# Round u slices dealt 5, 8, 8, a block's exponentials between the two last of a round, value products by turns and decay columns over four strips

## What is computed

```python
p_pool, gq, gk, gv, gg, gz_f, gz_b, aq, ak, av = _split_proj(h @ w_in)
la_f = _gla_log_decay(gz_f, gla_w_f, gla_b_f)      # log_sigmoid(gz_f @ w + b) / 16, gz_f and gz_b 16 columns each
y_attn = softmax over keys, then p @ v             # 8 heads, 2 key heads, window of 3 blocks and a cached one
mix = jnp.concatenate([y_pool, y_gla, y_attn], axis=-1)
x = x + gt1 * (mix @ w_out)
h2 = _rmsnorm(x, n2) * (1 + sc2) + sh2
# PEER: q = h2 @ wq; scores with subkeys; top 16 of 256 pair sums for each of 8 heads
gates = jax.nn.softmax(top_v, axis=-1)
act = gelu(einsum('td,tkd->tk', h2, u[experts]))
x = x + gt2 * einsum('tk,tkd->td', gates * act, v[experts])
```

## Time and profile before

| | |
|---|---|
| median of 3 runs | 3841.5 us (3837.81 to 3842.62) |
| the profiled execution | 3839.85 us |
| its span | 3838.0 us |
| PE busy | 3654.0 us, 95% |
| DVE, POOL, ACT busy | 2597.6, 1635.7, 699.3 us |
| mean granted clock | 0.983 |

### The profile page before, as it was taken

The page is one execution under the profiler, slowest core; times in us unless marked ns, Lnnn a source line. Parts: engine busy times, 40 slices in busy tenths (PEclk is TensorE's granted clock), DMA queues, the critical chain, the costliest instruction groups (busy, mean ns, idle before and its releaser), DMA issues. The chain is left out here.

```text
span 3838.0 us, 39960 instructions
## 1 busy us (share of the span) xinstructions
PE 3654.0 (95%) x13726; PEld 2084.1 (54%) x13726; DVE 2597.6 (68%) x6024; ACT 699.3 (18%) x1575; POOL 1635.7 (43%) x1498
## 2 busy tenths in 40 slices
PE   5888989999999999999989899899999999999997
PEld 3456776655555555554455567665555555555543
DVE  7784879977667667677624748899777555565444
ACT  1152366300000000000013425661000000000000
POOL 0210155466566544444402003554877564444330
PEclk9989999999999999999999999999999999999999
DMA  6323045799999999999830122558999999899774
GB/s 270 104 90 116 19 141 149 253 368 389 381 369 377 379 376 371 376 375 361 347 125 2 68 105 73 148 152 299 407 410 410 379 346 368 341 357 356 293 299 156
DMA packets 365049, 1026.96 MB, mean 268 GB/s; under 512 B 30352, under 2 KB 132016, under 8 KB 364208
## 3 DMA queue, kind: packets, MB, share of 16 engines
q0 software_dynamic: 147456, 536.94, 36.5%
q1 hardware_dynamic: 118352, 436.07, 29.7%
q10 hardware_dynamic: 99040, 51.40, 4.9%
HBM read 965.07 MB, written 59.22 MB: 267 GB/s over the span
## 5 line engine op out<-in xcount | busy, mean ns | idle before, releaser
L1860 PE MATMUL ps<-colsT,arena 128*128 128x384 f32 x4096 | 1370.1, 489 | 4.3 <-DMA arena<-in_peer_ut 4.3
L1860 PEld LDWEIGHTS ps<-colsT,arena 128*128 128x128 f32 x4096 | 780.6, 191 | 585.9 <-issue 104.1
L1896 PE MATMUL ps<-arena 128*128 128x512 f32 x1536 | 676.5, 592 | 0.0
L1388 POOL DMA_INDIRECT proj<-in_peer_u,eidx x336 | 476.5, 1418 | 240.3 <-DVE modbc L1573 106.0
L1388 POOL DMA_INDIRECT proj<-in_peer_v,eidx x335 | 359.9, 1074 | 316.4 <-DVE colsT L1584 217.2
L1896 PEld LDWEIGHTS ps<-arena 128*128 128x128 f32 x1536 | 291.8, 190 | 345.2 <-issue 317.6
L1374 POOL TENSOR_SCALAR x<-iota,modbc 128x128 f32<-128x128 f32 x192 | 145.3, 772 | 692.2 <-ACT modbc L1699 550.2
L1573 DVE CUSTOM_DVE_ANT_0 proj<-proj,rows 128x1024 f32<-128x1024 f32 x336 | 399.6, 1223 | 57.7 <-DMA proj<-in_peer_u,eidx 55.7
L1584 DVE SCALAR_TENSOR_TENSOR colsT<-proj,modbc,colsT 128x1024 f32<-128x1024 f32 x330 | 409.6, 1286 | 14.2 <-DMA proj<-in_peer_v,eidx 14.1
L1388 POOL DMA_INDIRECT modbc<-in_peer_v,eidx x177 | 200.4, 1132 | 325.8 <-DVE colsT L1584 259.7
L1896 PE MATMUL ps<-arena,rows 128*128 128x512 f32 x768 | 337.8, 592 | 0.0
(11 more groups left out here) (293 smaller groups left out, 3736.8 us busy)
## 6 DMA issues: line engine op xcount, KB each, us to landing
arena<-in_peer_ut SPq DMA_DIRECT2D x256, 512.0 KB, 6.8
arena<-in_peer_v SPq DMA_DIRECT2D x256, 512.0 KB, 6.7
gmat_d<-arena ACTq DMA_DIRECT2D x24, 2048.0 KB, 10.1
arena<-gmat_d SPq DMA_DIRECT2D x64, 768.0 KB, 9.0
proj<-in_w_adaT SPq DMA_DIRECT2D x51, 512.0 KB, 9.3
modbc<-in_w_adaT SPq DMA_DIRECT2D x19, 512.0 KB, 9.0
rows<-in_w_adaT SPq DMA_DIRECT2D x18, 512.0 KB, 3.5
arena<-in_w_in SPq DMA_DIRECT2D x2, 4224.0 KB, 16.3
```

Of the source, the lines that this page charges most:

```text
L1388: pool.indirect_dma_start(ring[slots[at]], None, tab, bass.IndirectOffsetOnAxis(ap=eidx[:, b * SLOTS + q:b * SLOTS + q + 1], axis=0)).then ...
L1860: mm = pe.matmul(ps[:, 2 + j % 2, 0:ND], utab[:, j % UR, k], hT[:, k, NG:T], start=(k == 0), stop=(k == KT - 1))
L1896: mm = pe.matmul(ps[:, Y_BANKS[2 * d + c2], :], wT[j % CR][:, d * P:(d + 1) * P], vtab[:, j % VR, c2 * 512:(c2 + 1) * 512], start=(j == 0) ...
```

## The change

Five edits.

1. `gz` is no longer made by `columns` but by `decay_columns`: k tile k goes to the strip of 32 output columns 32 (k % 4), so that four partial sums over two k tiles each stand in the four quarters of PSUM's partitions. `gzT` and `gw2` are 128 partitions high; `gw2` holds the weights four times, so the logits' matmul adds the four parts.
2. `values` takes the key blocks in the outer loop and the two heads in the inner one, and waits once for both heads' turned probabilities.
3. `G_U` deals 5, 8, 8 slices: round 1 gains one after step 6; round 2 has one after step 6 and none after step 3; round 3 loses the one after step 3. All 21 stay.
4. `exps(k)` stands between the two gelus of a round's last step.
5. In the routing of the first block, `residual(2)`, `mean(2)`, `normed(2)` come after steps 2, 4, 5 (before: 1, 2, 3), `residual(3)` after step 8 (7), and `mean(3)` after step 9 (8).

```diff
+                def decay_columns():
+                    free("gz")
+                    for seg, (t0, m) in enumerate(SEGS):
+                        for k in range(KT):
+                            r = slice(32 * (k % 4), 32 * (k % 4) + 32)
+                            mm = pe.matmul(ps[r, banks("gz")[seg], 0:m], w_b[:, k, 0:32], hT[:, k, t0:t0 + m],
+                                           start=(k < 4), stop=(k >= 4))
+                    mm.then_inc(u_mm, 1)
...
-                        mm = pe.matmul(ps[:, 6 + dr, 0:m], gw2[0:32, dr * P:(dr + 1) * P], gzT[0:32, t0:t0 + m], start=True, stop=True)
+                        mm = pe.matmul(ps[:, 6 + dr, 0:m], gw2[:, dr * P:(dr + 1) * P], gzT[:, t0:t0 + m], start=True, stop=True)
...
-                    for g in range(2):
-                        i = 2 * p + g
-                        pe.wait_ge(pt_sb, i + 1)
-                        for n, (kt, mk) in enumerate(keys[b]):
+                    pe.wait_ge(pt_sb, 2 * p + 2)
+                    for n, (kt, mk) in enumerate(keys[b]):
+                        for g in range(2):
+                            i = 2 * p + g
...
-        G_U = {1: (4, 5, 7, 7), 2: (-1, 1, 2, 3, 4, 5, 7, 7), 3: (-1, 1, 2, 3, 4, 5, 6, 7, 7)}
+        G_U = {1: (4, 5, 6, 7, 7), 2: (-1, 1, 2, 4, 5, 6, 7, 7), 3: (-1, 1, 2, 4, 5, 6, 7, 7)}
...
-                    if step == 1:
+                    if step == 2:
                         residual(2)
-                    if step == 2:
+                    if step == 4:
                         mean(2)
-                    if step == 3:
+                    if step == 5:
                         normed(2)
-                    if step == 7:
+                    if step == 8:
                         residual(3)
-                    if step == 8:
-                        mean(3)
+                mean(3)
                 normed(3)
...
-                        for _ in range(G_U[k].count(step)):
+                        for i in range(G_U[k].count(step)):
                             gelu(j)
                             j += 1
-                    exps(k)
+                            if step == G_STEPS - 1 and i == 0:
+                                exps(k)
...
-    d["gw2"] = gw
+    d["gw2"] = np.tile(gw, (1, 4, 1))
```

More of the change, by code:

```diff
@@ L442, in t_dst @@
             if n == "gz":
-                return gzT[0:32, t0:t0 + w]
+                return gzT[:, t0:t0 + w]
             if n == "gq":
@@ L482, in _ @@
                     sp.wait_ge(n1_turned, KT)
-                for dst, src in ((gw2[0:32], a["gw2"][l]), (ckT, a["ckT"][l]), (cvr, a["cv"][l])):
+                for dst, src in ((gw2, a["gw2"][l]), (ckT, a["ckT"][l]), (cvr, a["cv"][l])):
                     sp.dma_start(dst, src).then_inc(gla_landed, 16)
@@ L759, in filler @@
                     if n == "gz":
-                        columns(n, w_b, 0, 32)
+                        decay_columns()
                     elif n == "gq":
@@ L866, in evac @@
                     else:
-                        w = 32 if n == "gz" else P
-                        act.activation(t_dst(n, 1), ps[0:w, bk, :], ACT.Copy, scale=GDK ** -0.5 if n == "gq" else 1.0).then_inc(u_act, 1)
+                        act.activation(t_dst(n, 1), ps[:, bk, :], ACT.Copy, scale=GDK ** -0.5 if n == "gq" else 1.0).then_inc(u_act, 1)
                 def exps(p):
@@ L1004, in evac @@
                     else:
-                        w = 32 if n == "gz" else P
-                        dve.tensor_scalar(t_dst(n, 0), ps[0:w, bk, 0:P], GDK ** -0.5 if n == "gq" else 1.0, None, ALU.mult).then_inc(u_dve, 1)
+                        dve.tensor_scalar(t_dst(n, 0), ps[:, bk, 0:P], GDK ** -0.5 if n == "gq" else 1.0, None, ALU.mult).then_inc(u_dve, 1)
                 def head_max(p):
```

## The result

The changed kernel takes 3814.94 us (median of 4 runs, 3810.74 to 3817.14), the kernel before beside it 3839.65 (3836.29 to 3842.62): ratio 0.9929, 95% interval 0.9917 to 0.994. That is 24.7 us less. The forecast was 3808, some 32 less, with a range of 3794 to 3824. Direction and range held; the gain came out 7 us smaller.

What follows compares the result with a forecast made beforehand. PE, busy 3654.0 of 3838.0 us, was taken as the bound, leaving its idle time and low clock to win. Rounds with routing -20.6, decay columns -7.7 and values -3.8 gave -32.1, so 3808.0 us, range 3794 to 3824.

Steps and rivals of the forecast that it cites:

- first block's routing: Before round 1: moved residual work fills PE's 2.01 us wait at the turn; -2.0 us per layer.
- round 1: Added slice behind step 6 and earlier exponentials remove PE's idle times and low clock; -5.8 us per layer.
- round 2: Waits behind step 6 and at the turn go, a new 4.6 wait in step 4 and 1.7 low clock come; -1.8 per layer.
- round 3 and the slices behind: One slice fewer, same new wait and low clock, later slices and pairs simply move up; -0.7 us per layer.
- attention, layer 0: gq begins earlier, -1.5 us after giving back 1.0 for low clock; values by turns give 1.0.
- attention, layer 1: gz in strips lets gq start 6.2 us earlier; values by turns give 2.8.
- as nearly three at once: Layer 1's gz: four column strips overlap almost threefold, so gz takes 3.0 us instead of 9.72.
- strict order: Rival, 8%: only neighbouring pairs of matmuls overlap, gz takes 4.3 us, values gain nothing; about 3813.
- The rounds alone: Rival, 14%: attention's gains are swallowed because DVE and ACT set its steps; 3821.
- The change does not do what it says: Rival, 2%: strips and heads run one after another as before, gz and values give nothing; 3821.
- Slower: Rival, 3%: without a slice ahead of step 4, ACT stays behind in steps 5 and 6 too; 3848.
- More than forecast: Rival, 13%: the new waits bring no low clock (-6.8) and values count fully (-5); 3796.

Runs made afterwards that it cites:

- first trace: Profiled execution of the changed kernel in its first measurement, whose runs had a median of 3814.94 us.
- second trace: Profiled execution, 3801.3 us, of the changed kernel measured again unaltered; the median of that measurement was 3815.36 us.
- Experiment 8: Changed kernel with ACT writing out gz ahead of step 0's exponentials: 3815.98 us, ratio 0.9933.
- experiment 12: Changed kernel with one slice moved from behind step 7 to behind step 3 in rounds 2 and 3, and value products undone: 3799.0 us, ratio 0.9892.
- Experiment 5: Changed kernel with the old deal of slices, 4, 8, 9, exponentials still between the gelus: 3800.7 us, ratio 0.9903.
- experiment 2: Kernel before with the new deal 5, 8, 8 alone, exponentials still behind both gelus: 3842.67 us, ratio 0.9998.
- Experiments 4: Changed kernel with the strips undone (all hunks of gz, `gzT` and `gw2` reversed): 3823.83 us, ratio 0.9945.
- experiment 3: Changed kernel with the value products undone, one head after the other again: 3817.53 us, ratio 0.9932.

## Why the prediction was right, and where it was off

The terms, forecast and read from the table for the changed kernel's two traces, both layers together:

| term | forecast | first trace | second trace |
|---|---|---|---|
| first block's routing | -4.0 | -4.4 | -4.4 |
| round 1 | -11.6 | -11.8 | -12.0 |
| round 2 | -3.6 | -1.8 | -4.6 |
| round 3 and the slices behind | -1.4 | +1.9 | -5.8 |
| attention, layer 0 | -2.5 | +0.3 | -4.3 |
| attention, layer 1 | -9.0 | -7.0 | -7.5 |
| sum | -32.1 | -22.8 | -38.6 |

**Right, to tenths:** the routing and round 1, where the idle times that the forecast named went away and left 0.35 at the last group. The waits, their releasers and lengths were read from the trace; 1.96 and 0.95 of low clock went with them. The sign "round 1 with five slices in about 105.3" did not follow from the sum beside it: 109.14 less 5.8 is 103.3, and 103.3 is what it took.

**Right in mechanism, off in size.** Round 2: the idle time of 4.62 is as forecast, but "the low level follows, at the same 1.7" was too low in most cases: in the six traces with a bare step 3 and the exponentials between the gelus, eight of the twelve rounds 2 measured 85.6 or 85.7, three 84.2 or 84.3, and one 82.8, where no low clock came. The term is mis-sized by up to 1.2 in each layer. I had carried over 1.74, where the other stretch in the same rows, at the end of round 1, had cost 2.91.

**The step that was wrong: "The slices and pairs behind it are bound by PE and move up as they are."** Round 3 itself became 0.4 shorter in each layer of the first trace, where 0.7 was forecast. The slices behind it hang on an expert tile too. Counted from the first of the seven slices it comes at 38.2 in layer 0 of the kernel before and at 39.4 in the changed kernel; over nine traces of layer 0 at 37.2 to 40.2. The two traces of the changed kernel, 39.4 and 38.0, lie on either side of the 38.2, so no run shows that the edit moved it. Nor is that excluded: in layer 0 the three traces with a slice behind step 3 have 37.2 to 38.2 and the six without 37.9 to 40.2, while in layer 1 the two groups don't part (38.3 to 39.0, and 37.4 to 39.6). In the first trace it costs 1.2 more of idle time and 1.5 of low clock behind it, 2.7 of the 3.3 by which "round 3 and the slices behind" missed there. The second trace (38.0, a wait of 1.73, no low clock) is free of it. The row before, an idle time of 1.90 for a transfer, already said that this place has no slack, and the forecast had no term for it. The forecast's own sign for this stretch came: the pairs in layer 0 begin 6.3 us earlier (first v slice at 758.92 for 765.18), not 9. But its reading, that each new wait then costs more than 6.3, fits round 2 alone (4.62 and 2.9); in round 3 it was 4.38 and 1.7. The rest is the expert tile and layer 0's attention.

**Layer 0's gz:** "PE has then been idle for some 5 us and starts low, for which I give back 1.0". Idle time was 4.11, the price 2.6 (11.50 for 8.92), and of -1.5 nothing was left. Experiment 8 shows that what is won there is passed on to the wait at 192 us, and no run shows it at the end of attention.

**Layer 1's attention:** counted from the turn of the keys gq begins 6.4 us earlier in both traces, 6.2 forecast. Of the other 2.8, for the values, 0.6 came in the first trace and 1.1 in the second. Over all traces the values are worth between nothing and 3.5 there (experiment 12).

**The deal as a whole** was forecast at -0.3 per layer with the exponentials in place. Experiment 5 puts it at about +5 per layer. Without them experiment 2 finds nothing, as forecast, so the two edits' effects don't add. The forecast weighed it together with the exponentials, which alone give 16 to 20; split, the deal's own term would have shown as a coin toss with the risk on one side: it takes four waits of about 3 for POOL away (12.7 in all before, 1.3 now) and brings four of 4.4 to 4.6, two of them for ACT and two half for ACT, half for DVE.

**Strips and values.** Forecast "as nearly three at once"; it is four. PE in 0.85 us at the low level in layer 0, changed and then before (busy us, records, granted clock):

```profile
120.55:121.40 0.85, 0.81 (x16) 0.50 0.00 0
```

```profile
120.58:121.43 0.85, 0.81 (x4) 0.50 0.00 0
```

Sixteen records of gz pass where four did: they start in fours, each four within 0.05 us, and 0.2 us later the next. That gz came to 3.3 and 3.9 us, not 2.1, is mostly low clock, which both layers have at this place, behind the wait ahead of step 0's scores. This settles the rival of strict order against it: matmuls into different strips do not overlap in neighbouring pairs only. The Trainium skill ("TensorE: Matmul & The Clock Gate", Part 3: Packing small matmuls, "What overlaps and what doesn't") says that a weight load runs under a matmul in flight only if the row groups differ. Here they are the same, and in the 3.40 us from 120.60 to 124.00 PE was busy throughout and its weight loads for 1.49 of them, so the measurement decides. The same part's "Measured speedup", 2.38 for three column strips, points the right way; these rows show 4 for four.

**The rivals.** "The rounds alone" (3821) lies outside the result's interval, and layer 1's attention, 203.1 to 206.1 in the three traces with neither edit, is 193.6 to 199.2 in all with both. Experiments 4 and 12 point the same way, with wide intervals. In layer 0 the rival holds for the first trace, whose attention gained nothing. "The change does not do what it says" falls with the fours of gz. "Slower" did not come: step 5 shows no wait behind step 4's in round 2. "More than forecast" (3796) is not the median, but the one execution at 3801.3 shows the way there: the same code, its mean granted clock 0.982 for 0.979, shorter by 10.7 us in the rounds and "3+" and by 5.1 in attention.

## What to carry to other kernels

Price each edit of an order by itself before summing, and then ask what the edits do to each other: here one moved step, the exponentials, gave all of the rounds' gain, and the new deal that came with it gave about half of it back. Filler work is matmuls that are ready early and can be put between steps that wait for other engines. When it is dealt, put it first where the longest wait for another engine stands (here behind the scores' copy), and last where it covers nothing (behind a last step that waits for nobody); moving one slice so in two rounds gave 21 us. And charge an idle time with the low clock that may follow it: idle times of 3 to 4.6 us here were followed by anything from nothing to 2.9 us of it, so the larger price belongs in the middle of the estimate.

## What the runs showed of the hardware that I had not expected

Four matmuls with 32 output columns each, in four strips of the output's partitions, start within 0.05 us and run at once: 16 records in 0.81 us, where 4 passed. Two heads by turns, in two halves, take 1.03 us for 16 records to the start of the next row, where one head after the other took 1.51.

The low clock is not a fixed function of the code: behind the same idle time of 3.44 us in round 2, PE's 16 records took 3.76 in one execution of the changed kernel and 3.38 in another, and 2.02 in the kernel of experiment 3, whose code is the same there. One code's executions span 3801.3 to 3817.1 us, as much as most of the effects that were looked for, so single traces can be compared only stretch by stretch, and a stretch only beside its spread.
